# Four 32x32 diagonal tiles in place of two 64x64 tiles for levels 4, 8 and 16 of the recurrent branch's triangular inverse

## What is computed

```python
def step(S, inp):
    r_t, w_t, k_t, v_t, a_t, b_t = inp
    sa = jnp.einsum('bhij,bhj->bhi', S, a_t)
    S = S * w_t[:, :, None, :] + sa[..., None] * b_t[:, :, None, :] + v_t[..., None] * k_t[:, :, None, :]
    y = jnp.einsum('bhij,bhj->bhi', S, r_t) if emit else None
    return S, y
```

## Time and profile before

| what | value |
|---|---|
| three timed runs | 3104.19, 3101.37, 3097.13 us (median 3101.37) |
| span of the profiled execution | 3091.2 us |
| median less span (launch and end, outside the span) | 10.2 us |
| instructions in the span | 61066, of which 25648 matmuls and as many weight loads |
| the four runs of the inverse stage | about 40 us each, from 256.6, 391.7, 529.0 and 660.1 us |

### The profile page before, as it was taken

One profiled execution on the slowest core, in us unless ns is written; L12 is line 12 of the kernel. 1 busy time (PEld: TensorE's weight loads), 2 busy tenths in 40 slices (PEclk: granted clock), 3 DMA queues, 4 the chain that ended last, 5 costly groups with the idle time before them and its releaser, 6 DMA issues. The chain is left out here.

```text
span 3091.2 us, 61066 instructions
## 1 busy us (share of the span) xinstructions
PE 2874.3 (93%) x25648; PEld 2134.9 (69%) x25648; DVE 1512.4 (49%) x2768; ACT 964.4 (31%) x2248; POOL 771.8 (25%) x977
## 2 busy tenths in 40 slices
PE   6989998999998998999999989998999798999999
PEld 4968787886563786764588856645888576458674
DVE  5654636454433854541464246427833774265552
ACT  2021213122432124551221137511212574112561
POOL 3312223130013430011222214225531432244000
PEclk8999999999999999999999989999999899999999
DMA  6230100001332112121211152020111311212100
GB/s 225 81 113 19 39 4 16 17 32 59 110 103 101 55 55 96 56 83 41 83 52 47 66 188 77 11 95 34 55 55 55 124 55 56 87 47 89 58 1 28
DMA packets 108049, 206.16 MB, mean 67 GB/s; under 512 B 21795, under 2 KB 25394, under 8 KB 107264
## 3 DMA queue, kind: packets, MB, share of 16 engines
q1 hardware_dynamic: 107504, 201.36, 18.6%
q0 software_dynamic: 272, 0.89, 0.1%
HBM read 186.91 MB, written 15.54 MB: 65 GB/s over the span
## 5 line engine op out<-in xcount | busy, mean ns | idle before, releaser
L665 PE MATMUL psum<-weights,h_t 128*128 128x256 f32 x1488 | 352.0, 379 | 0.8 <-ACT p_u_u L749 0.8
L665 PEld LDWEIGHTS psum<-weights,h_t 128*128 128x128 f32 x1488 | 279.6, 190 | 38.5 <-ACT p_u_u L749 1.2
L1299 DVE TENSOR_REDUCE neg_max<-psum 128x1 f32<-128x768 f32 (+1 forms) x192 | 159.8, 864 | 220.4 <-PE psum L1169 174.8
L665 PE MATMUL psum<-z_l,x_tiles 128*128 128x256 f32 x816 | 192.8, 379 | 0.0
L665 PEld LDWEIGHTS psum<-z_l,x_tiles 128*128 128x128 f32 x816 | 155.0, 190 | 21.1
L1862 PE MATMUL psum<-weights,q_l 128*128 128x512 f32 x384 | 166.5, 592 | 0.0
L760 ACT ACTIVATE square<-psum 128x512 f32<-128x512 f32 (+1 forms) x80 | 45.0, 565 | 378.5 <-DVE psum L1017 242.0
L1190 PE MATMUL psum<-eye,prob 128*128 128x128 f32 x832 | 135.9, 286 | 11.3 <-DVE prob_t L1317 3.9
L1346 POOL TENSOR_TENSOR z_l<-z_l,inv_total 128x128 f32<-128x128 f32 x80 | 31.9, 399 | 428.7 <-DVE inv_total L1310 428.7
L1264 ACT ACTIVATE prob<-psum,neg_max 128x768 f32<-128x768 f32 (+1 forms) x160 | 129.7, 816 | 18.6 <-DVE neg_max L1299 12.4
L1862 PEld LDWEIGHTS psum<-weights,q_l 128*128 128x128 f32 x384 | 72.2, 190 | 87.1 <-issue 87.1
(11 more groups left out here) (445 smaller groups left out, 6175.9 us busy)
## 6 DMA issues: line engine op xcount, KB each, us to landing
weights<-in_ada_w_dram SPq DMA_DIRECT2D x30, 2048.0 KB, 8.0
weights<-in_a_w_in_dram SPq DMA_DIRECT2D x10, 2048.0 KB, 8.7
weights<-in_b_w_in_dram SPq DMA_DIRECT2D x8, 2048.0 KB, 9.2
weights<-in_c_w_in_dram SPq DMA_DIRECT2D x8, 2048.0 KB, 9.1
weights<-in_w_in_dram SPq DMA_DIRECT2D x6, 2048.0 KB, 7.7
x_aside<-x_tiles SPq DMA_DIRECT2D x24, 512.0 KB, 2.6
x_tiles<-x_aside SPq DMA_DIRECT2D x4, 3072.0 KB, 12.8
weights<-in_a_w_out_dram SPq DMA_DIRECT2D x4, 2048.0 KB, 8.0
```

The source lines that it names most:

```text
L665: last = pe.matmul(dst, lhs[:, k, :], rhs[k // 2][:, k % 2, :], start=k == 0, stop=k == KH - 1)
L1299: last = dve.tensor_reduce(neg_max[:, i % 4, m:m + 1], score(i, m, 0, keys), AX, ALU.max, negate=True)
```

## The change

A constant `QUAD = 32` is added. In `products`, the helper that issues all matmuls of the inverse stage, levels 4, 8 and 16 use tiles of 32x32 in place of 64x64: for each chunk there are four calls where there were two, one for each diagonal 32x32 block of the two heads. Weights shrink from 64x64 to 32x32, the moving operand from 64 (or 32) columns to 32 (or 16). The parts of PSUM off the diagonal blocks aren't written at these levels; they keep the zeros of level 2. Levels 2 and 32 and all other engines stay as they are.

```diff
+QUAD = 32
...
                 width = CH if half is None else CH // 2
+                size = QUAD if 4 <= m <= QUAD // 2 else CH
                 for c in range(a, e):
-                    for h in range(2):
-                        s = slice(64 * h, 64 * h + 64)
-                        out = pr.bank(bank)[s, width * (c - a):width * (c - a) + width]
-                        right = rhs[s, d, c, :]
+                    for g in range(P // size):
+                        s, at = slice(size * g, size * g + size), size * (g % (CH // size))
+                        out = pr.bank(bank)[s, width * (c - a) + at * width // CH:][:, 0:size * width // CH]
+                        right = rhs[s, d, c, at:at + size]
                         if half is not None:
                             out = out.rearrange("p (b m) -> p b m", m=m)
                             right = right.rearrange("p (b two m) -> p b two m", two=2, m=m)[:, :, int(half), :]
-                        last = pe.matmul(out, lhs[s, d, c, :], right, start=True, stop=True)
+                        last = pe.matmul(out, lhs[s, d, c, at:at + size], right, start=True, stop=True)
                 return last
```

## The result

The changed kernel takes 3200.19 us (median of four runs, 3199.17 to 3203.50), the kernel before 3099.25 us (four runs, 3096.72 to 3104.19): ratio 1.0339, 95% interval 1.0322 to 1.0356. It is 101 us slower, where 39 us faster was forecast, and outside the range. The profiled execution's span is 3201.7 us against 3091.2, 110.5 more. That execution itself took 3203.5 us, 1.8 more than its span, and so did every other run whose span is listed; the 10.2 us between median and span before is therefore mostly the spread between executions and not launch and end, and the forecast of 3062 us carried it along.

A forecast was written before the change was run, and what follows sets the result against it. TensorE was taken to bound the inverse stages: 8.40 - 4.52 - 0.35 = 3.53 us saved a level, 42 us over 12 levels, less 2.2, about 39.5. Forecast 3062 us beside 3101.4; range 3055 to 3125.

The forecast's parts named there:

- What bounds the kernel before: Four inverse stages of about 40 us: TensorE busy throughout, so whatever it saves is saved; 160 us of 3091 at stake.
- Part (1): Levels 4, 8 and 16: calls double, still 144 turns a level; 32-column loads cut each from 58.3 to 31.4 ns.
- (2): Four 32x32 tiles run side by side, four pairs a turn, needing 28 ns; a level takes 4.52 us.
- the turn: One load and one matmul on every TensorE tile in use; 58.3 ns before, set by the load's columns.
- Parts (3) to (5): Waits for ScalarE's copy cost 0.35 us a level, tile-size changes 2.2 us in all; other engines get the same instructions.
- the 3073 us for a turn of 36 ns: Upper end of the likeliest case's own range, which starts at 3055 us for 28 ns.
- instructions arrive too slowly: Rival: TensorE's instruction packets take 1.9 to 2.9 us each, 2 to 55 us slower, 3125 us in the middle; chance 0.23.
- packets end to end: Sign of the instruction rival: its queue's packets end to end, stretches of 40 us or more, waits marked as issue.
- the pace is that of records: Rival: each load-matmul pair costs 29.2 ns whatever its size, 16.8 us a level, 101 us more, 3202 us; chance 0.12.
- No change: Rival: only two 32x32 tiles go side by side, 9.0 us a level, 3109 us; chance 0.10.
- slower issue: Rival: TensorE issues at 5 to 7 ns an instruction, 5.8 to 8.1 us a level, 3072 to 3098 us; chance 0.13.
- The clock: Expected sign: stretches of 30 us instead of 40, with TensorE's granted clock still in full.

The follow-up runs named there:

- Experiment 1: Kernel before, but at levels 4, 8 and 16 the 64-row tiles load only 32 of 64 weight columns, same instruction count; 3098.96 us, ratio 1.0013.
- experiment 5: Kernel before, 64x64 tiles, both operands read as bfloat16 at levels 4, 8 and 16, 288 instructions a level; 3056.28 us, ratio 0.9881.
- 3: Changed kernel, but at levels 4, 8 and 16 only every second chunk is multiplied, 576 instructions a level; 3106.33 us in one run.
- 6: Changed kernel, 32x32 tiles, both operands read as bfloat16 at levels 4, 8 and 16, 576 instructions a level; 3104.06 us, ratio 1.0033.
- experiment 2: Kernel before, but at levels 4, 8 and 16 each 64x64 tile is two calls with 64x32 tiles, 1152 instructions a level; 3207.16 us, ratio 1.0353.
- experiment 7: Changed kernel plus 12 long matmul calls ahead of level 8, into a PSUM bank that nothing reads; 3247.3 us in one run.
- experiment 8: Kernel before, bfloat16 operands at levels 4, 8 and 16, GpSimd's and ScalarE's results written rounded to bfloat16; 3061.69 us, ratio 0.9883.
- experiment 9: Kernel before, bfloat16 operands with rounded writes at levels 4 and 8 only, level 16 in float32; 3070.96 us, ratio 0.9904.

## Why the prediction was wrong

**What bounds the kernel before.** Half right. TensorE does set the end of the stage, and no other engine takes over: the other three are busy as long as before, within 1 us a stage, in every run. But "TensorE is busy for all of it" was read as "the array is the limit". The array and the supply of instructions were level with each other: 58.3 ns for four instructions are 14.6 ns each, 3.73 us for 256, and the packets come every 3.7 us. Experiment 1 shows the second limit directly. The profile of the kernel before had a hint of it, 5.3 us in the whole run in which line 3018 waited for issue, nine times:

```profile
  issue: 5.3, 9
```

**Part (1) and (2), the turn.** Right as a statement on the array. 64 loads of 32x32 in 0.64 us, and bursts of 128 pairs in 1.13 us, 32 turns of 35 ns with the steps' ends among them, against 31.4; four small tiles do go side by side. The loads last 100 to 109 ns at the full clock and mostly 152 at the lower one, where about 110 was said:

```profile
L3020 PEld LDWEIGHTS psum<-rwkv_work,x_tiles x1536: 100/152/155, 264.7 to 796.4; 32*32 32x32 f32 x192
```

The step that failed is the one from the turn to the level: "a level is 144 x 31.4 = 4.52 us". It needs an instruction every 4 ns over 1152 instructions, and that pace holds for at most the packet in use and the next. The burst of the earlier trace rows, which gave the forecast its pace, was 32 matmuls and as many loads, a quarter of a packet: it can show what the array can do, not what it is fed. In place of 4.52 us a level costs about 16.6 us, 4.5 packets of 3.7 us each: the stages grew by 26.5 us on average, 8.8 for each of three levels, where 3.5 less was forecast. (A small slip in the sum changes nothing: the 3073 us for a turn of 36 ns come out nearer 3069, since 8.40 - 5.18 - 0.35 is 2.87 us a level.)

**Parts (3) to (5).** Of no weight in the changed kernel: the waits for ScalarE came to 0.4 us in the first stage, once, as before, because TensorE was late itself. Waits for ScalarE of up to 0.4 us each appear where fewer instructions are to be fed: five times in the first stage of experiment 5, three times in those of 3 and 6. The price of changing tile size was not measured by itself; experiment 2, whose tiles keep their 64 rows throughout, costs as much, so at least the change of rows is small beside the rest.

**The rival "instructions arrive too slowly"** had the mechanism, the place and the direction. Of the signs it was to be known by, two are what the profile shows, stretches over 40 us and waits marked as issue; the third, packets end to end, is not, since a packet is on its way for 1.06 of every 3.7 us. Two things in the rival were wrong. Its chance was 0.23, held down by a stock of some packets. And its price for a packet was taken from other small transfers, 1.9 to 2.9 us; it is 3.7. From a burst's start to the landing it is 1.25 + 1.07 = 2.3 us, inside those bounds; what the rival left out are the 1.4 us from the landing to the first instruction. With 3.7 us a packet the rival's own sum is 1152 / 256 x 3.7 = 16.65 us a level, 8.25 more than now, 99 us over 12 levels; measured 101 by the medians, 105.8 inside the stages of the two profiled executions. The lower clock behind the gaps is large enough for the excess of 6.8: in the first stage the last 294 matmuls, of level 32 and the products before it, took 10.9 us at a granted clock of 0.60, where 29.2 ns each would be 8.6. That is 2.3 us; in the other three stages 292, 304 and 274 matmuls took 11.7, 11.1 and 10.7 us, 3.2, 2.2 and 2.7 too many, some 10 in all. No run separates it. The range took in only the lower half of this rival, up to 3125.

Of its two readings of the Trainium skill, Runtime: NRT & Kernel Launch, section Instruction fetch mechanics, the blocks of 256 instructions agree with the bursts of 253 to 255; the memory of 2048 instructions that would have sunk the rival disagrees with experiment 7, where one packet came in 12 us of pause and 298 to 540 instructions ran behind it; "two lines" agrees with it.

**The rival "the pace is that of records"** gives nearly the same time (3202 us; 16.8 us a level), because 29.2 ns a pair is 14.6 an instruction, but not by its mechanism: starts don't come evenly, they come 4.4 ns an instruction apart in bursts (6.7 at the lower clock) and then not at all. Its count was right since the supply is in truth a pace of records, averaged over 256 of them. By the 25 ns floor of TensorE: Matmul & The Clock Gate in the Trainium skill, section Back-to-back issue gap, 128 pairs would need an estimated 3.2 us; on four tiles side by side they took 1.13.

**No change, and slower issue:** neither happened. Four tiles do overlap, and within a burst at the full clock instructions start 4.4 ns apart, not 5 to 7. Experiments 1, 3 and 6 say when the time stays nearly that of before: when the count of instructions stays.

**The clock.** The prediction took it to stay in full. It fell to 0.50 in or right behind the first full burst of each of the four stages. Among the bursts that cost little, since the next packet wasn't there anyway (experiment 1 has nearly the same period at the full clock); behind them it cost perhaps the 10 us above.

## What to carry to other kernels

Count TensorE's instructions as a resource of their own. Here a float32 call is two loads and two matmuls, 256 instructions come in 3.7 us, and so any stretch of this kernel longer than the two packets at hand that needs fewer than 14.5 ns for each is bound by the supply, whatever a smaller tile saves. Here a change that halved a tile's time and doubled its count doubled the time of its levels. A short burst in a trace shows the speed of the array but not the supply: to price a smaller tile, first run the old count of instructions with less work in each. And where a stretch sits at exactly this pace with TensorE busy all the time, fewer instructions are what helps, not cheaper ones: one pass in a narrower type gained 35 us here (experiment 8); larger tiles should help for the same reason, but were not tried.

## What was not expected of the hardware

- A packet of 256 TensorE instructions takes 3.7 us from burst to burst though its transfer occupies a DMA engine for 1.06 us and the other queues are all but idle; 1.4 us of it lie between the packet's landing and its first instruction. Mean periods are 3.71 to 3.85 us over seven kernels, at the full and at the lower clock.
- Only one packet is fetched ahead: in none of four pauses of some 12 us did more than one start (experiment 7).
- After such a gappy stretch the granted clock can stay at 0.50 for almost 20 us of work without a gap (experiment 9); in another stage of the same execution it was some 6 us. What decides between them stays open.
